# LRU stage of a hybrid decoder layer: the gate phase of the next tile issued between the scan steps of the current one

## The reference

```
u = rmsnorm(h, pre_g);  p = u @ w_in
q, k, v, g_att, x_lru, g_lru = split(p)                 # widths 1024 each
att = rmsnorm(stick_breaking_attention(q, k, v)) * silu(g_att)
xc = conv_b + causal depthwise conv of width 4 over x_lru
r = sigmoid(xc @ gate_a + b_a);  i = sigmoid(xc @ gate_x + b_x)   # 16 blocks of 64x64
a = exp(8 * r * log_sigmoid(lambda));  b = sqrt(1 - a*a) * (i * xc)
h_t = a_t * h_(t-1) + b_t                                # scan over time, per channel
lru = rmsnorm(h_t) * silu(g_lru)
out = h + rmsnorm(concat(att, lru) @ w_out, post_g)
```

## Time and profile before

| | |
|---|---|
| runs shown | 6033.63 us median of 2 (5989.6 and 6077.65) |
| profiled execution | 5988.73 us, span of its slowest core 5987.6 us |
| spans of the eight cores | 5960.8 to 5987.6 us |
| mean granted clock of TensorE, by core | 0.919 to 0.924 |
| busy: ScalarE / TensorE / VectorE / POOL | 4673.2 / 4173.9 / 2286.6 / 365.1 us |
| LRU stage in the span | first PX at 994.32 us, last small norm at 2201.03 us |

### The profile page before, as it was taken

The page is one execution under the profiler, slowest core; times in us unless marked ns, Lnnn a source line. Parts: engine busy times, 40 slices in busy tenths (PEclk is TensorE's granted clock), DMA queues, the critical chain, the costliest instruction groups (busy, mean ns, idle before and its releaser), DMA issues.

```text
span 5987.6 us, 82700 instructions; the slowest of 8 cores (5960.8 to 5987.6 us)
## 1 busy us (share of the span) xinstructions
PE 4173.9 (70%) x19280; PEld 1656.8 (28%) x19280; DVE 2286.6 (38%) x4921; ACT 4673.2 (78%) x9693; POOL 365.1 (6%) x590
## 2 busy tenths in 40 slices
PE   5888883555555557777777777777777777777587
PEld 3455552222222222222222222222222222222133
DVE  2222224666666653333333333333233333333244
ACT  4444445666666659999999999999999999999711
POOL 0000000111111100000000000000000000000133
PEclk9999997777777769999999999999999999999889
DMA  6332223111111120010010010010010000000244
GB/s 189 103 103 100 91 96 102 34 36 36 36 36 36 39 95 1 1 44 1 1 43 1 1 44 1 1 43 1 1 44 1 13 31 1 1 1 1 67 140 131
DMA packets 172304, 261.02 MB, mean 44 GB/s; under 512 B 47040, under 2 KB 126272, under 8 KB 167616
## 3 DMA queue, kind: packets, MB, share of 16 engines
q1 hardware_dynamic: 171840, 255.73, 12.6%
HBM read 179.68 MB, written 76.02 MB: 43 GB/s over the span
## 4 chain that ended last, share of the span: by engine, by line
ACT 51%; PE 26%; issue 13%; DMA 5%; DVE 3%; POOL 1%; ACTq 1%; SPq 0%; DVEq 0%; POOLq 0%
ACT E L141 21%; ACT Lb L141 17%; PE PK L144 5%; PE Z L144 4%; PE PV L144 4%; ACT Wt L141 3%; PE PC L144 2%; PE PG L144 2%; PE O L144 2%; PE PX L144 2%; PE TP L148 2%; DMA xt<-xs 1%; ACT xlb L141 1%; PE YL L144 1%; ACT At L141 1%
## 5 line engine op out<-in xcount | busy, mean ns | idle before, releaser
L154 DVE TENSOR_TENSOR SL<-SL,Lb 128x512 bf16<-128x512 bf16 (+3 forms) x2304 | 928.5, 403 | 2021.3 <-ACT Lb L141 1902.9
L141 ACT ACTIVATE E<-Z 128x512 f32<-128x512 f32 (+3 forms) x2368 | 1673.8, 707 | 18.5 <-PE Z L144 12.9
L141 ACT ACTIVATE Wt<-Z 128x512 bf16<-128x512 f32 (+3 forms) x2368 | 1674.6, 707 | 1.9 <-PE Z L144 1.4
L141 ACT ACTIVATE Lb<-E 128x512 bf16<-128x512 f32 (+3 forms) x2240 | 1667.4, 744 | 3.5 <-DVE E L154 2.9
L144 PE MATMUL Z<-Lb,cbf_s 128*128 128x512 bf16 (+3 forms) x2368 | 867.2, 366 | 793.3 <-ACT Lb L141 776.8
L144 PE MATMUL O<-Wt,Vh 128*128 128x512 bf16 (+3 forms) x2368 | 865.2, 365 | 87.3 <-ACT Wt L141 41.2
L144 PE MATMUL Z<-Qh,KT 128*128 128x512 bf16 (+3 forms) x2368 | 869.7, 367 | 18.8 <-DMA Qh<-Qs 18.8
L144 PE MATMUL Z<-SL,cbf_s 128*128 128x512 bf16 (+3 forms) x2304 | 844.0, 366 | 0.0
L144 PEld LDWEIGHTS Z<-Lb,cbf_s 128*128 128x128 bf16 x2368 | 227.4, 96 | 1801.5 <-issue 1800.5
L144 PE MATMUL PK<-uT,Wb1a 128*128 128x256 bf16 (+2 forms) x3264 | 495.3, 308 | 81.6 <-ACT kst L141 45.3
L144 PEld LDWEIGHTS O<-Wt,Vh 128*128 128x128 bf16 x2368 | 228.9, 97 | 700.8 <-issue 682.9
(11 more groups left out here) (90 smaller groups left out, 4192.7 us busy)
## 6 DMA issues: line engine op xcount, KB each, us to landing
xt<-xs SPq DMA_DIRECT2D x130, 512.0 KB, 6.2
stg<-w_in SPq DMA_DIRECT2D x12, 2048.0 KB, 11.6
KT<-KTs SPq DMA_DIRECT2D x8, 2080.0 KB, 9.1
Vh<-Vs SPq DMA_DIRECT2D x8, 2080.0 KB, 11.7
KTs<-kst SPq DMA_DIRECT2D x16, 1024.0 KB, 4.2
Vs<-vst SPq DMA_DIRECT2D x16, 1024.0 KB, 4.2
xr<-xs SPq DMA_DIRECT2D x32, 512.0 KB, 5.0
y<-ot SPq DMA_DIRECT2D x32, 512.0 KB, 3.3
```

What stands on the lines that cost most here:

```text
L141: self.S.op("act", lambda: self.nc.scalar.activation(out=out, in_=in_, func=func, **kw), r, w)
L154: self.S.op(e, lambda: self._v(e).tensor_tensor(out=out, in0=in0, in1=in1, op=op), r, w)
```

## The change

The stage's tile function becomes `mk_tile(ti)`, which issues nothing and returns five closures: `A1`, `A2` (both as before), `Bpre` (the eight square roots), `Bchunk(cc)` (all that the scan phase does for one chunk, its carry included) and `Bpost` (the norm and the DMA to `Ls`). A driver issues the gate phase of tile 0, and then for each tile m its `Bpre`, `A1(0)` of tile m+1, and per chunk: `Bchunk(cc)` of tile m, up to two uT steps of tile m+2, `A1(cc+1)` and `A2(cc)` of tile m+1. uT of tiles 0 and 1 are both built before the loop. `PS` gets the bank that the second `PC` had.

```diff
-        PCs = [es.enter_context(pst(f"PC{i}", [128, 512], F32)) for i in range(2)]
+        PCs = [es.enter_context(pst("PC0", [128, 512], F32))] * 2
...
-        PS = PG
+        PS = es.enter_context(pst("PS", [128, 512], F32))
...
-        bPCs = [PBuf() for _ in range(2)]
-        bPR, bPI, bPG = (PBuf() for _ in range(3))
-        bPS = bPG
+        bPCs = [PBuf()] * 2
+        bPR, bPI, bPG, bPS = (PBuf() for _ in range(4))
...
-        def lru_tile(ti, pend):
-            def pop():
-                if pend:
-                    pend.pop(0)()
+        def mk_tile(ti):
...
-            A1(0)
-            for cc in range(NCH):
-                if cc + 1 < NCH:
-                    A1(cc + 1)
-                A2(cc)
-            for cc in range(NCH):
-                k.act(Vt[:, cc, :TW], Vt[:, cc, :TW], AF.Sqrt, r=[bVt[cc]], w=[bVt[cc]], scale=0.25)
-            for cc in range(NCH):
+            def Bpre():
+                for cc in range(NCH):
+                    k.act(Vt[:, cc, :TW], Vt[:, cc, :TW], AF.Sqrt, r=[bVt[cc]], w=[bVt[cc]], scale=0.25)
+
+            def Bchunk(cc):
+                p = cc % 2
                 k.tt("dve", Vt[:, cc, :TW], T1[:, cc, :TW], Vt[:, cc, :TW], ALU.mult,
                      r=[bT1[cc], bVt[cc]], w=[bVt[cc]])
                 k.scan(Hs[:, cc, 1:1 + TW], At[:, cc, :TW], Vt[:, cc, :TW], Hs[:, cc, 0:1],
                        r=[bAt[cc], bVt[cc], bHs[cc]], w=[bHs[cc]])
-                pop()
-            if nq:
-                for cc in range(NCH):
-                    p = cc % 2
+                if nq:
                     k.act(out_my(hsq[:, p, :QW]), hmy(cc), AF.Square, r=[bHs[cc]], w=[bhsq[p]])
                     for q in range(nq):
                         k.mm(PS[:, q:q + 1], hsq[:, p, q * 128:(q + 1) * 128], onesb[:, 0:1], cc == 0 and q == 0,
                              cc == NCH - 1, r=[bhsq[p], bonesb], w=[bPS])
                     k.stt("dve", out_my(lst[sl][:, cc, :QW]), hmy(cc), lgh(cc), out_my(Gsg[:, cc, :QW]), ALU.mult, ALU.mult,
                           r=[bHs[cc], bder, bGsg[cc]], w=[blst[sl]])
-                    pop()
+                k.act(Hs[:, cc, 0:1], Hs[:, cc, TW:TW + 1], AF.Identity, r=[bHs[cc]], w=[bHs[cc]])
...
+        nt = len(tiles)
+        TL = [mk_tile(ti) for ti in range(nt)]
+        ut.emit(0)
+        if nt > 1:
+            ut.emit(1)
+        TL[0]["A1"](0)
+        for cc in range(NCH):
+            if cc + 1 < NCH:
+                TL[0]["A1"](cc + 1)
+            TL[0]["A2"](cc)
+        for m in range(nt):
+            pend = []
+            if m + 2 < nt:
+                ut.load(m + 2)
+                pend = ut.steps(m + 2)
+            nxt = TL[m + 1] if m + 1 < nt else None
+            TL[m]["Bpre"]()
+            if nxt:
+                nxt["A1"](0)
+            for cc in range(NCH):
+                TL[m]["Bchunk"](cc)
+                for _ in range(2):
+                    if pend:
+                        pend.pop(0)()
+                if nxt:
+                    if cc + 1 < NCH:
+                        nxt["A1"](cc + 1)
+                    nxt["A2"](cc)
             while pend:
-                pop()
...
+                pend.pop(0)()
+            TL[m]["Bpost"]()
```

More of the change, by code:

```diff
@@ L674, in lru_tile @@
                           r=[bHs[cc], bder, bGsg[cc]], w=[blst[sl]])
-                    pop()
-            while pend:
-                pop()
[L678 to L694, removed]
+                k.act(Hs[:, cc, 0:1], Hs[:, cc, TW:TW + 1], AF.Identity, r=[bHs[cc]], w=[bHs[cc]])
+            def Bpost():
+                if nq:
+                    k.cp("dve", sst[:, 0:nq], PS[:, 0:nq], r=[bPS], w=[bsst])
+                    k.ts("pool", sst[:, 2:2 + nq], sst[:, 0:nq], 1.0 / D, EPS, ALU.mult, ALU.add, r=[bsst], w=[bsst])
+                    for q in range(nq):
+                        k.tt("pool", rl[:, j0 + q:j0 + q + 1], sst[:, 2 + q:3 + q], nhalf, ALU.pow, r=[bsst, bcst], w=[brl])
+                    S.dma("sp", Ls.rearrange("c p t -> p c t")[:, :, j0 * 128:j0 * 128 + QW], lst[sl][:, :, :QW],
+                          reads=[blst[sl]], writes=[bLs], dsem=lsem[sl])
@@ new lines, in mk_tile @@
+            return dict(A1=A1, A2=A2, Bpre=Bpre, Bchunk=Bchunk, Bpost=Bpost)
+        nt = len(tiles)
[26 more added lines that the diff above has]
+                    nxt["A2"](cc)
+            while pend:
+                pend.pop(0)()
+            TL[m]["Bpost"]()
```

## The result

| | before | after |
|---|---|---|
| median of the runs | 6025.97 us (10 runs, 5982.48 to 6093.28) | 6707.52 us (11 runs, 6620.95 to 6724.99) |
| ratio | | 1.114 (95% interval 1.108 to 1.120): slower |
| profiled execution, span | 5988.73, 5987.6 us (core 5) | 6618.36, 6617.0 us (core 1) |
| spans of the eight cores | 5960.8 to 5987.6 us | 6584.2 to 6617.0 us |
| mean granted clock by core | 0.919 to 0.924 | 0.883 to 0.886 |

The forecast was 6690 us (6400 to 6800). The forecast was added onto the profiled execution before, so its like is the profiled execution after: that lies 69 us under the sum (6687 us).

What follows compares the result with a forecast made beforehand. The prediction took waits in the LRU stage, with no engine saturated, as the bound. Fifteen longer tile periods (+664), the narrow last tile (+16) and tile 1's uT (+18) added to 5988.7 gave 6687, about 6690 us; range 6400 to 6800.

Steps and rivals of the forecast that it cites:

- The signs: Expected LRU-stage traces: periods 115 to 121 us, scans 13 to 16 us apart, VectorE and ScalarE near 43% busy.
- the prologue: Before the first A1: building tile 1's uT there, with nothing beside it, costs +18 us once.
- the narrow tile: Last tile: its gate phase joins tile 15's scans, costing between 0 and 23 us, taken as +16.
- the turn: Between tiles: 12.3 us from tgt(7) to the first Square; with the second table load, +10.0 us a tile.
- Square to PX: Within a chunk: PX starts 0.62 us after Square, over PS; 2.51 us in chunks holding a transpose.
- A chunk with TensorE at half throughout and no uT step: Start-to-start waits of one LRU-stage chunk at TensorE's half level sum to 13.6 us.
- one with a transpose: Four chunks per tile hold a transpose, delaying PX by 1.9 us each: +7.6 us a tile.
- a chunk at full: The same chunk's waits with TensorE at its full clock level sum to 10.8 us.
- the ring: LRU stage: PX(cc+1) behind PS(cc), scan(cc) behind Gsg(cc-1) make gate and scan work run in turn; 13.6 us a chunk.
- The clock's share of the ring: TensorE at half level at every PX, full from PC on in two chunks of seven: 118 us a tile.
- At no cost: Claimed free: xt loads, single PC bank, PS's own bank, POOL's powers and the Hs carries beside PS.
- The overlap: Rival: LRU stage bound by ScalarE at 51.5 us a tile, kernel about 5675 us, -5%; chance 5%.

Runs made afterwards that it cites:

- one place cut: Changed kernel with A1(cc+1) issued ahead of Bchunk(cc): 6571.43 us; or with tt and scan issued one chunk ahead: 6437.83 us.
- the run with more filler: Changed kernel plus 24 unused matmuls after each PG and 5 after each PS: 6511.97 and 6740.61 us, no ratio given.
- the late carry alone: Changed kernel with only the Hs carry moved behind A2(cc): 6621.22 us, ratio 1.101 to the kernel before.
- two experiments: Changed kernel with tt and scan issued one chunk ahead: 6437.83 us; the same with A1(cc+1) also issued first: 6174.62 us.
- the last kernel: Changed kernel with A1(cc+1) first, scans one chunk ahead, carry behind A2(cc), A1(0) before the roots, tile 1's uT spread over tile 0's gate phase: 5784.81 us.
- both cuts and the late carry: Changed kernel with A1(cc+1) issued first, tt and scan one chunk ahead, and the carry behind A2(cc): 5866.16 us, ratio 0.973 to the kernel before.

## Why the prediction was right

**The mechanism.** It was read from the order of issue, and each link is in the rows: PS released by the Square in 56 of 56 chunks, PX 0.05 us behind it, the Square released by the scan, the scan behind Gsg. Shown by cutting it: from 114.7 us, one place cut gives 105.3 or 101.3 us, both 84.4, both with the carry out of the way 63.0, with the same computation in all of them. The moved uT steps taken away leave 109.4, the clock held up leaves 97 to 101.5, the banks alone make 75.1 of 73.7. What each cut leaves was not foreseen: the first ranges of the three were missed, each by a shorter ring that the traces then showed.
The Trainium skill (PSUM — Partial Sum Buffer, Engine vs sequencer instructions) says that the queues of ScalarE and VectorE are strict FIFOs and that matmuls start in program order. The 6.89 us in front of a PS of 0.19 us, with a ready PX behind it, are what that means for this kernel.

**The signs.** The forecast also named what the traces should show. Periods of 112.3 to 116.2 us reach into the low end of its 115 to 121, the Squares of the middle chunks are 12.3 to 15.7 us apart (13 to 16), PX is 0.05 us behind PS (0.06), and VectorE and ScalarE are busy 44% and 46% (43%). Two were off: the clock is 0.68 and not 0.5 to 0.6, and xlb waits 3.5 us for PX only in the chunk without a uT step, 0.9 to 2.4 in the others, where ScalarE has uT work of its own.

**The terms.** Right within the reading: the prologue (+17.4, forecast +18, in part by luck: by core the stretch takes 76.4 to 83.4 us after and 63.1 to 65.6 before, to the first roots' load), the narrow tile (+16.0, +16), the turn (12.1, 12.3), Square to PX 0.61 (0.62). A chunk with TensorE at half throughout and no uT step took 13.46 us (1478.10 to 1491.56 us; the sum said 13.6), one with a transpose 15.68 (1447.97 to 1463.65; 15.5), a chunk at full 10.7 (10.8, in the run with more filler). Within the transpose chunk two small errors stand against each other: Square to PX was 2.80 and not 2.51, since the carry waits 0.18 us for `lst` and holds up `ub`; the ring's other steps were 0.1 us shorter in sum.

**The mis-sized term.** The clock's share of the ring. The forecast put PC at full in two of seven chunks and PX at half in all, 3.67 us from PX to xlb. In tiles 2 to 14 PC is at full in 50 of 91, 3.8 of seven, which is 2.0 us a tile less. And PX took 2.8 to 3.6 us, where 1.89 is full level and 3.58 half: in most chunks the level rises on the way, and PX to xlb is 3.48 us in the mean, 1.3 us a tile less. The period is 114.2 and not 118: 15 periods make 55 us of the 69 by which the profiled execution lies under the sum. The other part is the start of the stage, 11.3 us earlier, and the small ends. How far the level shifts with a small offset is seen in the late carry alone, where with `ub` 0.38 us earlier PC is at full in 84 of 91.

**At no cost**, as costed: the loads, POOL, the banks (these last for the reason given at their run). The Hs carry was put at nothing, as lying beside PS; it delays PX by some 0.4 us per transpose chunk there (2.80 from Square to PX, 2.41 in the late carry alone), and it was what kept two experiments from their gain.

**The rivals.** The overlap (5675 us) was ruled out for the issue order of this change, and rightly; with the order repaired it is real, and its rest is the turn of a tile: in the last kernel 16.5 us from tgt(7) to tgt(0) (1511.26 to 1527.79) against 6.6 for a chunk, with 2 x 1.28 us of table loads and 4.3 us of roots. The forecast of 51.5 us a tile for that case took ScalarE's busy time alone and no wait; the best measured is 59.8, with ScalarE busy 80% of it.
The Trainium skill (Perfetto Trace Analysis, Optimization Strategy) says that interleaving regimes may improve performance. The runs have both outcomes of it: +11.4% with the ring in the issue order, -3.8% without it and with the turn and the first tile improved.

## What to carry to other kernels

Before two phases are interleaved on engines that work in program order, write the new order out for each engine and follow every wait across them, the smallest instructions too (here two one-column matmuls and a one-column copy): if the waits close a cycle per chunk, the phases run one after the other, however idle the engines are. Issue the next phase's independent matmuls ahead of this chunk's consumers, run the scan a chunk ahead, and put small late consumers (column sums, carries) behind the long work of their engine. Look at what a wait is really for, too: the carry waited for readers of columns that it doesn't write, since the dependencies are kept per slice. A lull that such a ring puts on TensorE is paid a second time in its clock; it goes away with the ring, while 6.6 us of filler matmuls in each chunk (1.24 and 5.34) bought less than the reordering.

## What the runs showed of the hardware

- One more semaphore wait on a matmul group, already fulfilled, took 0.11 us: from the start of xlb to PC are 0.85 us against 0.74, in the run with the banks changed and in the kernel before.
- POOL's power on 128x1 elements takes 0.55 us after the change and took 1.53 us before, when `tt` and `scan` of VectorE ran back to back beside it. From POOL's timelines, after and before:
```profile
1410.07 0.55 POOL L154 TENSOR_TENSOR ss<-ss,cst_s 128x1 f32<-128x1 f32 x1
```
```profile
1417.14 1.53 POOL L154 TENSOR_TENSOR ss<-ss,cst_s 128x1 f32<-128x1 f32 x1
```
  In the kernel with both cuts and the late carry, where VectorE is busy 77%, it takes 0.55 to 0.82 us. No run isolates the cause; that they share something is a guess.
- TensorE, 16 fillers a chunk: behind lulls of 2.16 and 1.24 us PX took 2.8 to 3.6 us (3.57 at 1505.29), at half for all or most of its time, though the window's clock was 0.85. With 24 and 5 fillers, behind one lull of 1.71 us, PX took 1.89, at full, and the window had 0.97; behind the lull of 4.23 us at a tile's first Square it took 3.57.
